# Down-projection of a convolutional GeGLU feed-forward layer in seven block products, its left sums made in the up-projection

## The reference, cut to what matters

```python
u = h @ w_up                                   # 512x2048 @ 2048x11264
c = conv_general_dilated(u, conv_w, ...) + conv_b   # causal, depthwise, width 3
gate, val = split(c, 2, axis=-1)
f = (gelu(gate) * val) @ w_down                # 512x5632 @ 5632x2048
x = x + rms_norm(f, g_ffn_post)
```

## Time and profile before

| | us |
|---|---|
| median of 3 runs (2088.2 to 2088.32) | 2088.27 |
| the profiled execution | 2087.82 |
| its span, first to last instruction | 2085.8 |
| matmuls on PE | 12774 |

### The profile page before, as it was taken

How to read it: one execution, slowest core, us unless ns; L and a number is a source line. 1 busy time by engine, 2 the same in 40 slices (tenths; PEclk the granted TensorE clock), 3 DMA queues, 4 the chain that set the end, 5 groups by cost and what they waited for, 6 DMA issues and landing times.

```text
span 2085.8 us, 31238 instructions
## 1 busy us (share of the span) xinstructions
PE 2049.3 (98%) x12774; PEld 1846.9 (89%) x12774; DVE 1255.2 (60%) x1608; ACT 925.0 (44%) x1477; POOL 0.7 (0%) x6
## 2 busy tenths in 40 slices
PE   8999999999999889999999999999999999999998
PEld 6888888888887789999999999999999888888886
DVE  5422533445346889887888888788887422323224
ACT  7422333445435655554555555555455322322222
POOL 0000000000000000000000000000000000000000
PEclk9999999999999999999999999999999999999999
DMA  8433222221646343243234224323424532452322
GB/s 314 142 116 116 89 90 70 82 68 60 236 145 239 121 144 120 92 139 135 92 112 162 92 93 152 121 92 120 154 92 148 175 127 100 152 207 93 99 98 95
DMA packets 188473, 265.54 MB, mean 127 GB/s; under 512 B 6494, under 2 KB 129534, under 8 KB 186156
## 3 DMA queue, kind: packets, MB, share of 16 engines
q1 hardware_dynamic: 187660, 258.31, 36.6%
q10 hardware_dynamic: 672, 5.24, 0.6%
HBM read 243.57 MB, written 23.89 MB: 128 GB/s over the span
## 4 chain that ended last, share of the span: by engine, by line
PE 94%; DVE 3%; ACT 2%; DMA 1%; issue 1%; DVEq 0%; SPq 0%; ACTq 0%
PE ring L1795 12%; PE ring L1797 12%; PE ring L1796 12%; PE ring L2056 10%; PE ring L2057 9%; PE ring L2058 9%; PE side L2056 4%; PE side L2058 4%; PE side L2057 4%; PE side L1796 4%; PE side L1797 4%; PE side L1795 4%; PE side L1871 1%; PE side L1844 1%; PE side L1829 1%; DMA raw<-in_w_mem_kv 1%
## 5 line engine op out<-in xcount | busy, mean ns | idle before, releaser
L1565 DVE TENSOR_TENSOR w_lo<-raw,w_hi 128x1024 fp32r<-128x1024 f32 x214 | 260.1, 1224 | 350.7 <-ACT w_hi L1114 307.1
L1286 DVE TENSOR_TENSOR w_lo<-raw,w_hi 128x512 fp32r<-128x512 f32 x256 | 169.6, 688 | 274.9 <-ACT w_hi L890 274.9
L2056 PE MATMUL ring<-s_hi,w_hi 128*128 128x256 f32 x1008 | 287.0, 285 | 8.5 <-ACT snaps L1172 5.2
L2057 PE MATMUL ring<-s_lo,w_hi 128*128 128x256 f32 x1008 | 286.6, 284 | 0.0
L2058 PE MATMUL ring<-s_hi,w_lo 128*128 128x256 f32 x1008 | 286.5, 284 | 0.0
L1565 DVE TENSOR_TENSOR w_lo<-q,w_hi 128x1024 fp32r<-128x1024 f32 x178 | 217.4, 1222 | 87.3 <-ACT w_hi L1107 83.1
L890 ACT ACTIVATE w_hi<-raw 128x512 fp32r<-128x512 f32 x256 | 151.6, 623 | 187.7 <-PE ring L1797 171.4
L1107 ACT ACTIVATE w_hi<-q 128x1024 fp32r<-128x1024 f32 x174 | 183.5, 1055 | 99.5 <-PE side L2058 55.1
L1114 ACT ACTIVATE w_hi<-raw 128x1024 fp32r<-128x1024 f32 x84 | 89.1, 1061 | 299.4 <-PE ring L1797 163.6
L2056 PEld LDWEIGHTS ring<-s_hi,w_hi 128*128 128x128 f32 x1008 | 194.6, 193 | 9.1 <-ACT snaps L1172 5.6
L2056 PE MATMUL ring<-a_hi,w_hi 128*128 128x256 f32 x688 | 195.9, 285 | 3.6 <-issue 3.3
(11 more groups left out here) (201 smaller groups left out, 4613.1 us busy)
## 6 DMA issues: line engine op xcount, KB each, us to landing
q<-in_w_up SPq DMA_DIRECT2D x65, 1024.0 KB, 4.9
raw<-in_w_down SPq DMA_DIRECT2D x84, 512.0 KB, 3.6
raw<-in_w_in SPq DMA_DIRECT2D x28, 1024.0 KB, 5.4
raw<-in_w_out SPq DMA_DIRECT2D x24, 1024.0 KB, 4.9
raw<-in_w_up SPq DMA_DIRECT2D x23, 1024.0 KB, 6.9
a_d<-c_val SPq DMA_DIRECT2D x44, 256.0 KB, 5.3
raw<-in_w_mem_kv SPq DMA_DIRECT2D x8, 1024.0 KB, 6.8
snaps<-a_d SPq DMA_DIRECT2D x28, 256.0 KB, 4.2
```

Of the source, the lines that this page charges most:

```text
L1286: dve.tensor_tensor(w_lo[:, s, q], raw[:, s, q], w_hi[:, s, q].bitcast(F32), ALU.subtract).then_inc(lo_done, 1)
L1565: dve.tensor_tensor(view[0], src, view[1].bitcast(F32), ALU.subtract).then_inc(hp_lo_done, 1)
L2056: pe.matmul(dst, hi, b_hi, start=first, stop=False, skip_group_check=True)
L2057: pe.matmul(dst, hi, b_lo, start=False, stop=False, skip_group_check=True)
```

## The change

The down-projection is cut as the up-projection is. Rows of `w_down` are taken in 22 pairs of 128 (row blocks 1 and 2), columns in two halves of 1024 (column blocks 1 and 2), tokens in two halves of 256. Each of four passes takes 22 pairs. Passes 0 and 1 make four products (P1, P5, P7, P3) for 512 of the 1024 columns of both halves, passes 2 and 3 the other three (P6, P2, P4) for the same columns. A step has two halves ("half-steps", each one of them a window): 12 and 12 matmuls of 512 columns in passes 0 and 1, 12 and 6 in passes 2 and 3. A product has two banks (two token tiles), so that a pass holds eight banks, or six. The weight sums: B12 + B22 (passes 0 and 1) and B12 + B22 + B11 (passes 2 and 3, two adds) are made by DMAs from POOL that add in SBUF; B12 + B11 and the sum for P4 are made by DVE. The left sums, of the activations, are made by DVE in the up-projection (`left_sums`, four operations on 128x256 in each chunk) and written to DRAM with the products, so that pairs come back as "items" of 128x1024 or 128x768. In a chunk, `c11` moves from step 7 to step 10, and some of the early chunks' work moves by a few steps.

```diff
+def pass_pair(d):
+    v, j = d // N_PAIRS, d % N_PAIRS
+    return v, (j if v % 2 == 0 else N_PAIRS - 1 - j)
...
+            def load_down(d):
...
+                if v < 2:
+                    sp.dma_start(seg(d, 3), w_down_d[k1, n2]).then_inc(twin_in[s], 16)
+                    sp.dma_start(seg(d, 0, 2)..., w_down_d[k1, :]...[:, :, n1]).then_inc(down_in[s], 16)
+                    sp.dma_start(seg(d, 2), w_down_d[k2, n2]).then_inc(down_in[s], 16)
+                else:
+                    sp.dma_start(seg(d, 1), w_down_d[k1, n2]).then_inc(twin_in[s], 16)
+                    sp.dma_start(seg(d, 0), w_down_d[k2, n1]).then_inc(down_in[s], 16)
...
+            for w in range(first_load, H_DOWN + N_DOWN - 8):
...
+                e = w - H_DOWN + 11
+                if e % 2 == 0 and 4 <= e // 2 < N_STEP:
+                    sp.wait_ge(hp_lo_done, H_DOWN + e - 6)
+                    load_down(e // 2)
...
+                b1 = H_DOWN + 6 * N_PAIRS
+                for w_back, rows_back in ((b1 + 2 * 6 + 1, (0, 1)), (b1 + 2 * 11 + 1, (2, 3))):
+                    if w == w_back:
+                        sp.wait_ge(hp_used, w + 1)
+                        for t in rows_back:
+                            sp.dma_start(x1_back_at[:, t, :], x1_d[t]).then_inc(x1_back, 16)
+                if w == b1 + 2 * 8 + 1:
+                    sp.dma_start(g_f[:, :], g_ffn_post.to_broadcast([P, D])).then_inc(g_f_in, 16)
...
+            def add_block(d, at, row, col, done):                      # POOL
+                pool.dma_start(seg(d, at), w_down_d[...], accum_op=ALU.add).then_inc(done[d % 4], 16)
+            def second(d):
+                pool.wait_ge(added_a[d % 4], 16 * (d // 4 + 1))
+                add_block(d, 1, 0, 0, added_b)
+            for d in range(N_STEP):
+                pool.wait_ge(twin_in[d % 4], 16 * (d // 4 + 1))
+                add_block(d, 3 if d < 2 * N_PAIRS else 1, 1, 1, added_a)
+                if d > 2 * N_PAIRS:
+                    second(d - 1)
+            second(N_STEP - 1)
...
+            def left_sums(c):                                          # DVE
+                combine(c_gate[:, 0, hi], c_val[:, 0, hi], c_val[:, 1, hi], ALU.subtract)
...
+                e = w + 4 - H_DOWN                                     # DVE, after(w)
+                if e >= -1 and e % 2 and e + 1 < N_DOWN - 4:
+                    if e + 1 < 4 * N_PAIRS:
+                        sums_a((e + 1) // 2)
+                if e >= 4 * N_PAIRS and e % 2 == 0:
+                    sum_t4(e // 2)
+                hp_to_lo(w + 4)
...
+                if w == w_at(0) or w == w_at(1):
+                    sum_f(w == w_at(1), "12a", 0)
+                    sum_f(w == w_at(1), "12a", 1)
+                if w == w_at(0) + 1 or w == w_at(1) + 1:
+                    n = w == w_at(1) + 1
+                    for m in range(2):
+                        sum_f(n, "22a", m)
+                        sum_f(n, "21a", m)
+                    sum_f(n, "12b", 0)
+                    sum_f(n, "12b", 1)
...
-            for w in range(H_DOWN + N_DOWN - 4):
+            for w in range(H_DOWN + N_DOWN - 8):
                 after(w)
+            for e in range(N_DOWN - 4, N_DOWN):
+                if e % 2 == 0:
+                    sum_t4(e // 2)
+                hp_to_lo(H_DOWN + e)
+            for i, t in enumerate(TAIL_T):                             # TAIL_T = (0, 2, 1, 3)
+                m = t % 2
+                dve.wait_ge(down_ready, i + 1)
+                if t < 2:
+                    for what in ("11", "12", "22", "21b"):
+                        sum_f(1, what, m)
+                else:
+                    sum_f(1, "21", m)
+                times_gain(TT + i, 1, t)
...
+            for d in range(N_STEP - 4):                                # PE
+                for half, names in enumerate((("p1", "p5"), ("p7", "p3")) if d < 2 * N_PAIRS else (("p6", "p2"), ("p4",))):
+                    operands(d, half)
+                    for name in names:
+                        for m in range(2):
+                            mm = down_product(d, name, m)
+                    mm.then_inc(hp_used, 1)
+            for m in range(2):
+                for half, names in ((0, ("p6", "p2")), (1, ("p4",))):
+                    for d in range(N_STEP - 4, N_STEP):
...
+                    mm.then_inc(down_ready, 1)
```

More of the change, by code:

```diff
@@ new lines, with stage_before, load_window @@
+ITEMS = left_items()
+ITEM_OF = {}
+for _i, (_w, _kind, _p, _slot, _free, _stage) in enumerate(ITEMS):
+    ITEM_OF.setdefault((_kind, _p), []).append(_i)
+ITEMS_AT = {}
+for _i, _item in enumerate(ITEMS):
+    ITEMS_AT.setdefault(_item[0], []).append(_i)
+def stage_before(i):
+    same = [k for k in range(i) if ITEMS[k][5] == ITEMS[i][5]]
+    return same[-1] if same else None
+def load_window(i):
+    last = stage_before(i)
+    return max(ITEMS[i][0] - 7, H_DOWN - 7 if last is None else ITEMS[last][0] + 1)
@@ L626, in build, with seg, blocks_in @@
[L626 to L634, removed]
+        raw_slots = [x.rearrange("p k n -> p (k n)") for x in
+                     (quarters[3][:, :, :], quarters[2][:, :, :], raw_q[0], raw_q[1])]
+        def seg(d, i, n=1):
+            return raw_slots[d % 4][:, i * BLK:(i + n) * BLK]
+        def blocks_in(d):
+            return down_in[d % 4], sum(32 if k < 2 * N_PAIRS else 16 for k in range(d % 4, d + 1, 4))
@@ new lines, in added, with block_sum_count, half_width, half_source @@
+        def added(d):
+            if d < 2 * N_PAIRS:
+                return added_a[d % 4], 16 * (d // 4 + 1)
+            return added_b[d % 4], 16 * sum(1 for k in range(d % 4, d + 1, 4) if k >= 2 * N_PAIRS)
+        def block_sum_count(d, name):
+            return d + 1
+        def half_width(e):
+            return BLK if e % 2 and e >= 4 * N_PAIRS else 2 * BLK
+        def half_source(e):
+            d, half = e // 2, e % 2
+            return seg(d, 2 * half, half_width(e) // BLK)
+        def half_at(e):
+            d, half = e // 2, e % 2
+            if d >= LATE:
+                first = 3072 * (d - LATE) + 2 * BLK * half
+                return [late[:, at:at + half_width(e)] for at in (first, first + 1536)]
+            return [w[:, e % 4, 0:half_width(e)] for w in (hp_hi, hp_lo)]
@@ new lines, in stage_sem, with f_at, f_row, w_at @@
+        def stage_sem(i):
+            where = ITEMS[i][5]
+            return stage_in[where], 16 * sum(1 for item in ITEMS[:i + 1] if item[5] == where)
+        bank_x, bank_y, bank_v, bank_w = side[0:2], ring[2:4], ring[0:2], side[2:4]
+        def f_at(n, m, what):
+            row, col = int(what[0]) - 1, int(what[1]) - 1
+            return (f0, f1)[n][:, m + 2 * row, col, :]
+        def f_row(n, t):
+            return (f0, f1)[n][:, t, :, :]
+        def w_at(v):
+            return H_DOWN + 2 * N_PAIRS * v + 2 * N_PAIRS - 2
@@ L2144, in _, with operands @@
[L2144 to L2149 removed]
+            def operands(d, half):
+                pe.wait_ge(hp_lo_done, H_DOWN + 2 * d + half + 1)
+                if half == 0:
+                    v, p = pass_pair(d)
+                    pe.wait_ge(a_lo_done, ITEM_OF["AB"[v // 2], p][v % 2 and len(ITEM_OF["AB"[v // 2], p]) - 1] + 1)
```

553 lines of the change are left out of this document (325 added, 228 removed).

## The result

| | before | after |
|---|---|---|
| median, us (4 runs each) | 2088.23 (2087.9 to 2088.32) | 2122.03 (2118.94 to 2126.52) |
| ratio | | 1.0164, 95% interval 1.0147 to 1.018 |
| the profiled execution, us | 2087.82 | 2126.52, the slowest of the four |

Forecast were 2063 us and a range from 2043 to 2106. The change makes the kernel 34 us slower, outside that range; the nearest case was rival (c), 2114 us.

A forecast was written before the change was run, and what follows sets the result against it. PE, busy for 98% of the span, was taken to bound the kernel. 2087.8 - 59.9 + 4.4 + 11 + 7 + 5 + 7 = 2062.3, as a median 2063 us, range 2043 to 2106.

The forecast's parts named there:

- rival (c): Passes 2 and 3: POOL's issues and the adds' latency are slower than taken, step 5.4 us, total 2114 us; chance 0.20.
- The matmuls removed, -59.9: Down-projection: 264 of 2112 matmuls go, at 0.2268 us each, saving 59.9 us.
- Up-projection and passes 0 and 1, cost 0: Added DVE sums in the up-projection and splits in passes 0 and 1 fit in idle time: 0 us.
- Rival (d): Up-projection: DVE at 83 + 4% makes PE wait, a third of 37 us, total 2075 us; chance 0.06.
- Pass ends, +4.4: Ends of passes 0, 1 and 2: PE waits for banks, 1.7, 2.0 and 0.7 us; bounds 0 and 3 x 5.5.
- Tail, +11: After the last matmul: DVE works through four token tiles, 16.1 us in place of 5.2, on the path.
- Last four steps, +5: Steps 84 to 87, taken half by half: PE waits for late weights, 5 us; bounds 1.4 and 15.
- Residual, +7: Pass 3: two 2 MB bursts of x1 and the gain delay weight loads, 7 us; bounds 0 and 13.
- The adding loads, +7: Passes 2 and 3: two adds in series stretch a step from 4.08 to 4.23 us, 7 us; bounds 0 and 77.
- A: An adding load's time from issue to landing, taken as 4.8 us: 4.2 plus 0.6 for the second operand.
- E: Time for which POOL is held by an adding load's issue, taken as 1.2 us, between 0.37 and 2.5.
- Rival (b): Passes 2 and 3: DMA engines bind, step 4.8 us, +33 in place of +7, total 2092 us; chance 0.14.

The follow-up runs named there:

- experiment 3: Changed kernel with no adding load in passes 0 and 1, where DVE makes B12 + B22 instead: 2125.3 us.
- experiment 1: Changed kernel with POOL's 132 loads copying instead of adding, same place, size and order: 2080.5 us.
- experiment 2: Changed kernel with the second add of passes 2 and 3 left out (B11 missing from one weight sum): 2055.9 us.
- experiment 5: Changed kernel with the two adds of passes 2 and 3 in parallel, the second into the place's fourth block without waiting: 2088.2 us.
- experiment 4: Changed kernel with DVE making all weight sums and no adding loads: 2063.87 us, ratio to before 0.988.
- experiment 7: Changed kernel with DVE sums instead of adds in passes 0 and 1, one adding load and two DVE sums a step in passes 2 and 3: 2073.58 us.
- experiment 8: Changed kernel, passes 0 and 1 kept, with one adding load and two DVE sums a step in passes 2 and 3: 2070.9 us, ratio 0.9908.
- experiment 9: Kernel of experiment 4 with x1 loaded back in eight pieces of 512 KB in place of two bursts of 2 MB: 2062.67 us, ratio 0.9873.
- experiment 6: Changed kernel without the residual: x1 is not loaded back in pass 3 (4 MB less on SP's queue): 2113.3 us.

## Why the prediction was wrong

**The matmuls removed, -59.9**: right, 264 fewer at a distance that is 0.227 us where PE doesn't wait (2104.22, 2104.45, 2104.68 in PE's timeline).

**Up-projection and passes 0 and 1, cost 0**: right, within the 0.8 us by which the down-projection begins later. PE is at 100% in the windows of the up-projection and of pass 0, DVE up from 82.6 to 86.7 us in 100. Rival (d) did not occur. That pass 0 would fill the DMA engines (1.05) was not in the prediction, which had summed no bytes for it; it happened to be harmless, as experiment 3 shows.

**Pass ends, +4.4**: at the end of pass 0 2.0 us (1.7 forecast), in after and in experiments 1, 2 and 5 alike. At the end of pass 1 PE waits 1.5 us for "12a" in experiments 1, 2 and 5 and 2.8 in after (2.0 forecast). At the end of pass 2 experiment 2 has 0.9 (0.7 forecast), after 5.9 in one wait for "11": there the sum stands on DVE behind weight sums that wait for adds. Without late adds the three come to the 4.4 us forecast, and the mechanism was right.

**Tail, +11**: right. DVE goes through four tiles, waits 1.22 us for the square in the two tiles with one sum, and ends at 2121.2:

```profile
2101.78 0.69 DVE L1912 TENSOR_TENSOR f<-ring,f 128x512 f32<-128x512 f32 x1
...
2108.03 0.69 DVE L1912 TENSOR_TENSOR f<-ring,f 128x512 f32<-128x512 f32 x1
...
2114.88 0.69 DVE L1912 TENSOR_TENSOR f<-ring,f 128x512 f32<-128x512 f32 x1
...
2118.72 2.48 DVE L2018 SCALAR_TENSOR_TENSOR f<-f,rstd,x_back_at 128x1024 f32<-128x1024 f32 x2
```

The starts of the second to the fourth tile lie 6.25 and 6.85 us apart (6.4 and 7.1 forecast), and from the last matmul to the end of the span it is 19.1 us, 10.8 more than before.

**Last four steps, +5**: experiment 2, where adds are hidden, has waits of 1.7 + 2.0 + 0.9 + 0.9, 5.4 us, there; after has 9.4 in all, slow matmuls included. Where DVE makes two or three sums a step (experiments 4 and 7 to 9) these steps lose 11 to 12 us.

**Residual, +7**: 8 to 10 us where the ring binds (experiment 6), and nothing that can be told where it doesn't (9). Right in size for after.

**The adding loads, +7, is the step that failed.** Pass 2 alone lost 30.9 us, and the middle of pass 3 23.9 without the bursts (experiment 6): some 55 us where 7 were forecast. The chain was the right one; two of its values were too small, and the engines' own limit was not in the term. These loads have, in pass 2:

```profile
q<-in_w_down SPq DMA_DIRECT2D x20, 256.0 KB, 5.4
raw<-in_w_down POOLq DMA_DIRECT2D x18, 256.0 KB, 6.6
q<-in_w_down POOLq DMA_DIRECT2D x16, 256.0 KB, 6.1
raw<-in_w_down SPq DMA_DIRECT2D x16, 256.0 KB, 5.2
```

So A is up to 6.6 and not 4.8, SP's plain load of B12 ("twin load") 5.3 and not 3.6; E is 0.875, less than the 1.2 taken. In T = (twin load + E + A + 3.1) / 3 that gives 5.3 us a step, and the 22 steps of pass 2 took 120.7, 5.49 each. With A and E right and the twin load at 3.6, T would be 4.7: each of the two values is worth some 0.6 us a step, and the prediction gave no surcharge at all to the plain load. With its series taken out the formula becomes (6.6 + 1.8 + 6.5 + 3.1) / 4 = 4.5, and experiment 5 has 4.56. It is not exact near its threshold: for experiment 1 it gives (3.9 + 0.5 + 4.0 + 3.1) / 3 = 3.8, under 4.08, and pass 2 still lost 5.5 us.

A was taken from plain loads where the DMA share is 0.5 or less, with a surcharge of 0.6 us for the second operand. But the change itself brings the engines near full. Rival (b) had the arithmetic for that: six units of 262 KB a step, 4.8 us, and the runs give 4.7 by measured price, and 2088.2 for its 2092 when the series is taken out. It was written down as a case of its own with 0.14, when its condition held in every case with two adds a step, and its consequence for the landing times in the chain was left out. Rivals (b) and (c) come together: the engines near full, late landings, and two of them in series in the ring. That (c)'s T of 5.4 lies so near is in part luck: it had E at 2.5 us for 0.875 and the twin load at 3.6 for 5.3, and the two errors cancel. Experiments 1, 2 and 5 show the cause from three sides: take away the adding, the second add or the series, and 40 to 72 of the 87.0 us go (passes' sums 459.2, 434.1 and 466.2 against 505.9).

**What no step had**: PE's clock. After pauses it ran for some matmuls at half speed, 18.7 us in after, 0.2 in pass 2 of experiment 2. In after the pauses cost more than their length: 18.7 us beside 67.8.

The Trainium skill's figure for a plain DMA from POOL (DMA: Bandwidth & Descriptors, "Anatomy of one DMA") gives 2.6 us for 256 KB, an estimate by its formula; experiment 1 has 2.8 us at least and 4.5 as a median. As a floor the runs come near it; as a latency in this kernel they don't. The Trainium skill (SBUF — State Buffer, the "DVE blocks DMA" trap) warns that a DVE operation in a 2-port mode keeps POOL from writing descriptors. The trace shows no such hold-up beside this kernel's two-input sums and splits: an add's issue takes 0.865 us at least, 0.875 as a median and 1.575 at most, with DVE busy for 49 to 81%.

Left open: how much less the slow matmuls would cost with the same pauses, since each pause brings both, and whether late landing comes of the engines' share alone. Whether a ring of more than four places would hide the series was not tried.

## What to carry to other kernels

Before a latency is taken from a trace for a chain that is to be short, sum the bytes of the new step over its new, shorter time: if the engines come out near full, latencies from the idle stretch don't hold, and "engines full" is a condition of all other cases, not a rival with a chance of its own. An adding DMA took 1.8 to 2 times the engine time of a plain one here, and two of them into one place, the second waiting for the first, were more than a ring of four places hid; a 128x512 sum on DVE took 0.69 us and beat it. When one resource is relieved, check the next one by its busy share: DVE at 97 of 98 us left nothing for a further gain, and POOL could not take a sum off it.

## What was not expected of the hardware

- An adding load takes 1.8 to 2 times the DMA engine time of a plain load's byte (96 or 93 us per MB of one engine against 47 to 52), and lands after 3.7 us at least, 6.6 as a median (the same loads without adding: 2.8 and 4.5).
- Its issue holds POOL for 0.875 us, that of a plain load 0.536.
- The two granted levels of PE's clock show in the distance between matmuls, 0.43 us for 13 matmuls right after a pause of 7.3 us, against 0.227.
- POOL's sum of 128x512 takes 1.67 us and makes DVE's sums beside it 1.01 in place of 0.69 us.
- The DMA share can pass 1 (1.05 from 1603 to 1720 us, in pass 0), while PE waits for nothing.
